# HGRN tiles beside the projections: where TensorE's level products, output rows and state steps stand among the projection groups, and when a tile's norm and carry are done

## The reference, cut to what matters

```python
h = _rms_norm(x, norm_g)
aq, ak, av, ag, hq, hf, hi, hg = jnp.split(h @ w_in, _split_points(), axis=-1)
```

```python
hq = silu(hq); f = lb + (1 - lb) * sigmoid(hf); logf = log(f); hk = 1 - f
def step(S, inp):                      # one chunk of tokens, per head
    b = jnp.cumsum(lfc, axis=1)
    decay = exp(where(tri, b[:, :, None] - b[:, None, :], -inf))
    att = einsum('bthd,bshd,btshd->bhts', qc, kc, decay)
    o = einsum('bhts,bshv->bthv', att, vc) + einsum('bthd,bhdv->bthv', qc * exp(b), S)
    S_new = exp(bC)[..., None] * S + einsum('bshd,bshv->bhdv', kc * exp(bC[:, None] - b), vc)
r = _rms_norm(o_hgrn, hgrn_norm_g) * silu(hg)
```

## Time and profile before

| what | us |
|---|---|
| median of 3 runs | 1795.5 |
| lowest and highest | 1792.37, 1800.49 |
| the profiled execution's own time | 1799.58 |
| its span, first to last instruction | 1797.8 |
| the sixteen steps in it, by TensorE | about 435 to 994 |
| next pass, TensorE's first matmul | 1004.36 |
| mean granted TensorE clock over the span | 0.964 of full |

### The profile page before, as it was taken

One profiled execution on the slowest core, in us unless ns is written; L12 is line 12 of the kernel. 1 busy time (PEld: TensorE's weight loads), 2 busy tenths in 40 slices (PEclk: granted clock), 3 DMA queues, 4 the chain that ended last, 5 costly groups with the idle time before them and its releaser, 6 DMA issues. The chain is left out here.

```text
span 1797.8 us, 25182 instructions
## 1 busy us (share of the span) xinstructions
PE 1609.2 (90%) x9156; PEld 1299.9 (72%) x9156; DVE 988.6 (55%) x2314; ACT 754.3 (42%) x1076; POOL 495.1 (28%) x637
## 2 busy tenths in 40 slices
PE   7799999997999999999999699999998378599998
PEld 5588888886877878788787466777776245377776
DVE  5322222254776676677666498888887341343332
ACT  4333333345445345444544466666666022221110
POOL 1323333333446545644654000000000210012121
PEclk9999999998999999999999699999999589899999
DMA  8433333453001101010110430100000845324342
GB/s 294 173 141 141 141 140 141 175 190 115 30 30 54 36 30 52 31 36 30 54 36 7 152 118 25 47 14 13 13 18 25 254 160 191 107 100 164 134 152 70
DMA packets 79827, 172.27 MB, mean 96 GB/s; under 512 B 9059, under 2 KB 15715, under 8 KB 79715
## 3 DMA queue, kind: packets, MB, share of 16 engines
q1 hardware_dynamic: 79714, 170.79, 27.7%
HBM read 114.13 MB, written 56.62 MB: 95 GB/s over the span
## 5 line engine op out<-in xcount | busy, mean ns | idle before, releaser
L92 PE MATMUL h_banks<-h_w_hi,h_x_hi 128*128 128x512 f32 x1088 | 435.1, 400 | 24.0 <-DVE h_x_lo L651 16.8
L94 PE MATMUL h_banks<-h_w_hi,h_x_lo 128*128 128x512 f32 x1088 | 426.6, 392 | 0.0
L93 PE MATMUL h_banks<-h_w_lo,h_x_hi 128*128 128x512 f32 x1088 | 426.3, 392 | 0.0
L92 PEld LDWEIGHTS h_banks<-h_w_hi,h_x_hi 128*128 128x128 f32 x1088 | 206.3, 190 | 66.6 <-DVE h_x_lo L651 17.2
L94 PEld LDWEIGHTS h_banks<-h_w_hi,h_x_lo 128*128 128x128 f32 x1088 | 205.8, 189 | 44.5
L93 PEld LDWEIGHTS h_banks<-h_w_lo,h_x_hi 128*128 128x128 f32 x1088 | 206.4, 190 | 40.6
L145 POOL TENSOR_TENSOR h_stage_or_levels<-h_stage_or_levels,h_qk_or_hgrn 128x128 f32<-128x128 f32 x192 | 107.4, 559 | 278.2 <-ACT h_stage_or_levels L589 278.2
L1078 ACT ACTIVATE p_scores<-p_scores,p_nmx 128x256 f32<-128x256 f32 (+15 forms) x128 | 153.1, 1196 | 6.2 <-DVE p_nmx L1129 5.9
L1214 PE MATMUL p_ops<-p_V,p_WT 128*128 128x128 f32 x1088 | 146.4, 280 | 8.8 <-ACT p_WT L1087 8.4
L1214 PEld LDWEIGHTS p_ops<-p_V,p_WT 128*128 128x128 f32 x1088 | 132.6, 193 | 15.8 <-ACT p_WT L1087 14.4
L1124 DVE CUSTOM_DVE_ANT_0 p_scores<-p_sps,p_zero 128x512 f32<-128x512 f32 x192 | 122.2, 686 | 15.9 <-PE p_sps L1188 15.7
(11 more groups left out here) (218 smaller groups left out, 2739.3 us busy)
## 6 DMA issues: line engine op xcount, KB each, us to landing
h_stage_or_levels<-in_w_in SPq DMA_DIRECT2D x32, 512.0 KB, 6.3
h_xs_sq_or_tok<-in_xT SPq DMA_DIRECT2D x17, 512.0 KB, 6.0
h_qk_or_hgrn<-in_x SPq DMA_DIRECT2D x17, 512.0 KB, 6.1
tmp_xh_s<-h_x_hi SPq DMA_DIRECT2D x17, 512.0 KB
tmp_xl_s<-h_x_lo SPq DMA_DIRECT2D x17, 512.0 KB
h_x_hi<-tmp_xh_s SPq DMA_DIRECT2D x17, 512.0 KB, 3.6
h_x_lo<-tmp_xl_s SPq DMA_DIRECT2D x17, 512.0 KB, 4.5
s_kc<-in_cache_k SPq DMA_DIRECT2D x32, 256.0 KB, 3.8
```

The lines of the kernel that those rows point to most:

```text
L92: eng.matmul(out, x_hi[:, k, :], w_hi[:, k, :], start=(k == 0), stop=False)
L93: eng.matmul(out, x_hi[:, k, :], w_lo[:, k, :], start=False, stop=False)
L94: mm = eng.matmul(out, x_lo[:, k, :], w_hi[:, k, :], start=False, stop=(k == KD - 1))
```

## The change

TensorE's list: the first half of group 1 now stands before `levels(t, 0)`, its second half before `levels(t, 1)`; `head_columns` stands before `levels(t, 2)`; group 2 is split around `levels(t, 2)`, and `out_rows(t, pt, 3)` is the last entry of the step, behind all of group 3.

VectorE's list: `carry`, the sum of squares (`o_sums`, split off `o_norm`) and `o_norm` of tile t-1 are done in step t, before and behind the first `keep_pairs`; `cumulate` and the first half of `differences` come before `keep_pairs(t, 3)`, the second half behind it. `carry` has a new wait, for all `out_rows` of its tile.

ScalarE's list: the gate of tile i is read in step t behind the exponentials of half 0, and no longer first in the step that uses it; the squares and the root of tile t-1 stand behind `inputs_q(i)`; the copy of the keys' rows stands behind `decays`, the value before the exponentials of half 0. The lists of GpSimd and SyncE are not changed.

```diff
@@ ScalarE, step(t, pt, more)
-                gate_input(t, pt)
                 inputs_q(i)
+                if t >= 1:
+                    o_stats(t - 1)
                 inputs_f(i)
+                q_columns(i)
+                decays(i)
                 act.wait_ge(s["kdT_ps"], t + 1)
                 after(act, s["gain_ps"], t)
                 act.activation(kd_tok, kps.rearrange("p h d -> p (h d)"), ACT.Copy).then_inc(s["kd_tok"], 1)
-                q_columns(i)
-                decays(i)
+                value_input(i, p)
                 if more:
                     exps(i, 0)
-                value_input(i, p)
+                gate_input(i, p)
                 if more:
                     exps(i, 1)
                     tile_decay(p)
-                o_stats(t)
@@ ScalarE, ahead of and behind the loop of steps
+            value_input(0, 0)
             exps(0, 0)
-            value_input(0, 0)
+            gate_input(0, 0)
             exps(0, 1)
...
                 step(t, t % 2, t < NP - 1)
-            gate_input(NP, 0)
+            o_stats(NP - 1)
@@ VectorE
-            def differences(i, t):
-                for hf in range(2):
-                    if t is not None:
-                        dve.wait_ge(s["av"], 4 * t + 2 * hf + 2)
-                        dve.wait_ge(s["kdT_ps"], t + 1)
-                    decay_differences(dve, half(bT, hf), lv[hf], all_levels, P).then_inc(s["diff"], 1)
+            def differences(i, t, hf):
+                if t is not None:
+                    dve.wait_ge(s["av"], 4 * t + 2 * hf + 2)
+                    dve.wait_ge(s["kdT_ps"], t + 1)
+                decay_differences(dve, half(bT, hf), lv[hf], all_levels, P).then_inc(s["diff"], 1)
+            def o_sums(t):
+                dve.wait_ge(s["o_sq"], t + 1)
+                dve.tensor_reduce(oss[:, 0], o_out..., AX.X, ALU.add).then_inc(s["o_ss"], 1)
...
             def carry(t, pt):
                 dve.wait_ge(s["gain_ps"], t + 1)
                 dve.wait_ge(s["ebc"], t + 1)
+                dve.wait_ge(s["av"], 4 * t + 4)
...
             def step(t, pt, more):
                 i = t + 1
+                if t >= 1:
+                    carry(t - 1, 1 - pt)
+                    o_sums(t - 1)
                 keep_pairs(t, 0)
+                if t >= 1:
+                    o_norm(t - 1)
                 keep_pairs(t, 1)
+                forget(i)
                 keep_pairs(t, 2)
-                forget(i)
+                if more:
+                    cumulate(i)
+                    differences(i, t, 0)
                 keep_pairs(t, 3)
                 if more:
-                    cumulate(i)
-                    differences(i, t)
-                o_norm(t)
-                carry(t, pt)
+                    differences(i, t, 1)
...
+            carry(NP - 1, 1)
+            o_sums(NP - 1)
+            o_norm(NP - 1)
@@ TensorE, step(t, pt)
                 group(i, p, 0)
+                group(i, p, 1, (0,))
                 levels(t, 0)
-                group(i, p, 1, (0,))
+                group(i, p, 1, (1,))
                 levels(t, 1)
                 out_rows(t, pt, 0)
-                group(i, p, 1, (1,))
+                head_columns(i, t)
+                group(i, p, 2, (0,))
                 levels(t, 2)
                 key_rows(t)
                 out_rows(t, pt, 1)
-                head_columns(i, t)
+                group(i, p, 2, (1,))
                 levels(t, 3)
                 out_rows(t, pt, 2)
-                group(i, p, 2, (0,))
-                out_rows(t, pt, 3)
-                group(i, p, 2, (1,))
                 group(i, p, 3, (0,))
                 gains(t, pt)
                 group(i, p, 3, (1,))
+                out_rows(t, pt, 3)
```

More of the change, by code:

```diff
@@ L761, in cumulate @@
                 dve.wait_ge(s["cumsum"], i + 1)
-            def differences(i, t):
-                for hf in range(2):
-                    if t is not None:
-                        dve.wait_ge(s["av"], 4 * t + 2 * hf + 2)
-                        dve.wait_ge(s["kdT_ps"], t + 1)
-                    decay_differences(dve, half(bT, hf), lv[hf], all_levels, P).then_inc(s["diff"], 1)
+            def differences(i, t, hf):
[5 more added lines that the diff above has]
+                dve.wait_ge(s["o_sq"], t + 1)
+                dve.tensor_reduce(oss[:, 0], o_out.rearrange("p (h v) -> p h v", h=H), AX.X, ALU.add).then_inc(s["o_ss"], 1)
             def o_norm(t):
-                o3 = o_out.rearrange("p (h v) -> p h v", h=H)
-                dve.wait_ge(s["o_sq"], t + 1)
-                dve.tensor_reduce(oss[:, 0], o3, AX.X, ALU.add).then_inc(s["o_ss"], 1)
                 dve.wait_ge(s["o_root"], t + 1)
@@ L776, in o_norm @@
                 dve.wait_ge(s["o_rs"], t + 1)
-                dve.tensor_tensor(o3, ops, oss[:, 2, :, None].broadcast_to([P, H, DV]), ALU.mult).then_inc(s["o_norm"], 1)
+                dve.tensor_tensor(o_out.rearrange("p (h v) -> p h v", h=H), ops, oss[:, 2, :, None].broadcast_to([P, H, DV]),
+                                  ALU.mult).then_inc(s["o_norm"], 1)
             def carry(t, pt):
@@ L791, in _ @@
             cumulate(0)
-            differences(0, None)
+            differences(0, None, 0)
+            differences(0, None, 1)
             def step(t, pt, more):
                 i = t + 1
+                if t >= 1:
+                    carry(t - 1, 1 - pt)
+                    o_sums(t - 1)
                 keep_pairs(t, 0)
+                if t >= 1:
+                    o_norm(t - 1)
                 keep_pairs(t, 1)
+                forget(i)
                 keep_pairs(t, 2)
-                forget(i)
+                if more:
+                    cumulate(i)
+                    differences(i, t, 0)
                 keep_pairs(t, 3)
                 if more:
-                    cumulate(i)
-                    differences(i, t)
-                o_norm(t)
-                carry(t, pt)
+                    differences(i, t, 1)
             dve.wait_ge(s["mask"], 1)
```

## The result

The change is slower: 1826.2 us (median of 4 runs) against 1793.9 of before beside it, ratio 1.018 with a 95% interval of 1.014 to 1.021. I had forecast 1777. The profiled execution took 1830.2 around a span of 1828.4, 30.6 more than before's span of 1797.8.

What follows compares the result with a forecast made beforehand. TensorE, busy in 90% of the span, bounds the kernel, so only its waits can be won. Steps save 24.5 us, the end gives back 6.0: -18.5 off the 1795.5 median gives 1777 us, range 1760 to 1798.

Steps and rivals of the forecast that it cites:

- TensorE's list, 32.4 us: TensorE's work in one step, laid out without waits from its start E, the first matmul of group 0: 32.4 us stay.
- The attention waits gone: TensorE's wait for VectorE's attention sums before `out_rows` 3, 1.34 us a step, is gone; `out_rows` 0 is covered too.
- Half 0 of the operands: GpSimd's operands, started at E - 1.95, end at 9.2; TensorE still waits 1.05 us a step at `levels` 0.
- an unbroken hold of 3.5 us: VectorE's half 1 differences keep GpSimd out in the middle of its half 0 work, adding 3.5 us to 7.67.
- my lower bound: GpSimd's loss beside VectorE's half 1 differences was bounded by 0 (slips in without loss) and 3.63 us.
- VectorE's half 1 differences to 4.1, mask 0 "covered": Run early in the next step, they take 3.63 us; the sum of squares ends near 9.7, before mask 0's 10.1.
- the 0.25 of slack at `out_rows` 0: The norm is ready at 13.95 us into the step, against 14.2 when TensorE reaches `out_rows` 0.
- Two more table loads cost nothing: ScalarE's gate Silu between the exponentials adds 2.6 us a step, ending about E + 1.8, before the differences' end at 4.1.
- Step 0 and the end: Step 0 saves 3.2 us; norm and gating behind the last matmul cost 6.0 us at the end.
- two engines take turns: Rival, chance 0.14: GpSimd gets in between VectorE's half 1 differences, which end at 9.4; 2.35 us more a step, 1833 us.

Runs made afterwards that it cites:

- experiment 2: The change plus one wait: GpSimd starts half 0 of the operands only when both halves of VectorE's differences are done; 1839.7 us, ratio to before 1.021.
- experiment 1: The change with VectorE's sum of squares of tile t-1 moved behind mask and sum of head 0; 1794.2 us, ratio to before 0.996.
- Experiment 4: The change with, in the last step only, `out_rows(t, pt, 3)` before `gains`, ScalarE's squares before its last `gate_input`, VectorE's norm before `carry`; 1826.8 us, ratio 1.011.
- experiment 3's first run: The change with GpSimd's operands held by a semaphore until the second of VectorE's 16 half 1 differences is done; 1816.6 us beside 1797.1 of before.
- the run behind the twelfth difference: As experiment 3's first run, but GpSimd is let in behind the twelfth half 1 difference, beside the last four; 1839.9 us beside 1800.3 of before.
- experiment 5: The kernel before with only TensorE's new order, other engines' lists unchanged and `out_rows(t, pt, 3)` still ahead of `gains`; 1845.1 us.

## Why the prediction was wrong, step by step

- **TensorE's list, 32.4 us**: right. `levels` 0 stood at E + 8.26, and the steps of three kernels at full clock are this sum and their waits: 35.83 (35.9), 34.08 (34.2), and 35.77 in experiment 2 (32.4 + 3.31 + 0.15 = 35.86).
- **The attention waits gone**: right, 1.34 a step. `out_rows` 3 does not wait in any run with the whole change.
- **Half 0 of the operands**: the step that failed. I took an unbroken hold of 3.5 us from rows 6, 7, 8 and 9, with half 0 ready at 9.2. It was ready at 6.25 and `levels` 0 did not wait. GpSimd lost 0.4, near my lower bound, and the price went to the other engine. My bounds were both for GpSimd; VectorE's half of the contention, in the forecast, stood at nothing ("of normal length"), though the rival had priced it.
- **VectorE's half 1 differences to 4.1, mask 0 "covered"**: wrong by that. They ended at 8.2, mask 0 ended at 14.9. The cover was less than I had said, too: of the delay up to 5.6 that it was to allow, 1.05 was TensorE's own wait at `levels` 0, which did not come. From the differences' end to that of the sum of squares took 5.7, and mask 0's place was 10.1, so it decides from about 4.4.
- **The wait that I did not list**: I watched mask 0 only as the start of `out_rows` 0. `levels` 1 wants it first, at 12.75, for its bank. Mask 0 started 3.7 late (13.8 instead of 10.1); less the 0.25 of slack at `out_rows` 0 that is 3.45, and it shows as the entries of 2.29 and 0.90, 3.5 with 0.15 for each.
- **Two more table loads cost nothing**: right as far as the exponential goes. It still began behind the differences, at 8.25.
- **Step 0 and the end**: 3.2 and 6.0 forecast; 3.7 and 6.3 measured. The step's 0.36 of `out_rows` 3 lies on the other side of `gains`, which is where I measure, and would account for the difference. Step 0 isn't known to that, though: in experiments 1 to 4, with the same list of TensorE up to there, its `gains` came between 463.5 and 467.7 us of the span, here at 463.6 and before at 467.3. Experiment 4 shows that 4.2 of the end came from where `out_rows` 3 and the work behind it stand.
- **The rivals**: "two engines take turns" is what happened, with a chance of 0.14 and 1833 against 1826. It had the differences' end at 9.4 (8.2 measured), because it made GpSimd's products count in full for VectorE, whereas a 128 x 128 one costs 0.26 of its 0.47 and a wide one 1.1 of its 1.3. And it had no clock in it, which took 10.3 us of the 32: without that the kernel would, by this account, have come to 1816. The two errors go opposite ways, so that its total came out near is in part luck. The rule that I cited with it (the Trainium skill, "SBUF — State Buffer", the section on two separate sides: whichever starts first has the port pair for the whole instruction) describes the change and experiment 3's first run, to about 0.1 us an instruction. It does not describe rows 6 and 7 or the run behind the twelfth difference, where GpSimd stood through the ends of several instructions of VectorE.
- **The range**, 1760 to 1798, left the full turns out. The evidence that I set against the rule, two places with one hold each, was too thin for 0.14: both had GpSimd arriving beside other VectorE instructions than the 128 x 128 ones, and in the change GpSimd was already at work. I had named this difference and not priced it.

## What to carry to other kernels

When two engines that disturb each other are moved into one stretch, price the disturbance for both, and then follow what is queued behind the one that loses: here about the same stretch, over 4 us, came with steps of 35.8, 34.1 or 33.2 us at full clock, by where one reduction, and then also the squares, the norm and the first output rows, stood in the lists. A row that shows contention holds for the instructions in it; before carrying it to others, look whether the newcomer finds the same shape running. And of an early result ask for every reader, the next writer of its bank among them.

## What the runs showed of the hardware

- VectorE's two-input differences and GpSimd's products, all in SBUF, alternate one by one. A GpSimd product goes from 0.46 to 0.51, a VectorE difference from 0.28 to 0.54 beside a 128 x 128 product and to 1.38 beside a 128 x 512 one.
- GpSimd arriving beside VectorE's last four differences waits for them all: 1.45 and 1.50 for a product of 0.46, VectorE not slowed, in two kernels. Arriving beside 128 x 128 ones it gets in at once, and turns that are going go on through the wider ones (0.68 and 0.73 instead of 0.42 in experiment 3's first run).
- The granted clock fell to its lower level in 10 of 15 steps around the end of one wait of 2.29, in 12 of 15 with one of 3.1 and in 13 of 15 with one of 3.3 (experiments 3 and 2), in every step with one of 3.7 (experiment 5), and in none with one of 1.7 (experiment 1) or with three of 1.2, 1.1 and 0.9 (experiment 3's first run, 36.0 us in every step). Since equal waits of 2.29 brought it in some steps and not in others, their length alone does not decide it; what does was not tried. So a wait of TensorE can cost more than its length: 2.29 and 0.90 cost a further 0.68 a step on the mean. The three short ones, 3.13 together, cost nothing on top (32.4 + 3.13 + 0.45 = 35.98).
